# Value products of the prompt moved to the spare columns of a transpose bank, in a one-core hybrid decoder layer

## What is computed

```
q, k, v, z_b, u, v_a, z_a, g_a, g_b = split(x @ w_in + b_in)        # 2048 -> 17408 columns
branch A: y_a = gelu(u) * (tril(w_s) @ layer_norm(gelu(v_a)) + b_s) * silu(z_a)      # chunks of 128
branch B: 3 dilated windows (128,1), (512,4), (2048,16) of 8 heads x 128, rotary q and k;
          o = softmax(q k^T / sqrt(128)) v per window, the three merged by their softmax weights
          y_b = o_b * silu(z_b)
merged = sigmoid(g_a) * (y_a @ w_o_a) + sigmoid(g_b) * (y_b @ w_o_b)
x <- layer_norm(2**0.25 * x + merged @ w_out)
```

## The kernel before, in words

| step | engine | work |
|---|---|---|
| 3 + 4i | TensorE | `prompt_scores(i)`: scores into the two banks of `scp` (lines 866, 868) |
| 4 + 4i | VectorE | scale, mask and maximum out of `scp` into `sc` (line 1583), maximum and its negative (lines 1640, 1574) |
| 4 + 4i | ScalarE | Exp of `sc` (line 1254) |
| 8 + 4i | VectorE | `normalise`: `sc` times the reciprocal sum (lines 1579, 1580) |
| 10 + 4i | TensorE | six transposes of `sc` into `turn` (line 830): four into bank 0 (half 0), two into columns 0 to 255 of bank 1 (half 1) |
| 11 + 4i | ScalarE | both halves copied to `pt` (line 1036) |
| 13 + 4i | TensorE | `prompt_out(i)`: six matmuls of `pt` with the values (line 878), into columns 0 to 127 of `scp` |
| 14 + 4i | VectorE | the product times the gate, into `zt`, which the profile calls `qkv` (line 1646) |

## Time and profile before

### The profile page before, as it was taken

One profiled execution on the slowest core, in us unless ns is written; L12 is line 12 of the kernel. 1 busy time (PEld: TensorE's weight loads), 2 busy tenths in 40 slices (PEclk: granted clock), 3 DMA queues, 4 the chain that ended last, 5 costly groups with the idle time before them and its releaser, 6 DMA issues.

```text
span 2398.1 us, 43888 instructions
## 1 busy us (share of the span) xinstructions
PE 2295.2 (96%) x17409; PEld 2245.2 (94%) x17409; DVE 1602.6 (67%) x2107; ACT 910.6 (38%) x1320; POOL 254.8 (11%) x458
## 2 busy tenths in 40 slices
PE   7999999999999999999988998999899989999997
PEld 7999999999999999999978998899889988999996
DVE  8677867867777776777747675676566656553435
ACT  5444444444444444444433233333333432332221
POOL 0100000000000000000023221221221110001000
PEclk9999999999999999999999999999899999999998
DMA  5443343433434334344368766866775573344333
GB/s 176 132 131 108 115 135 96 130 110 114 133 100 128 106 118 131 102 148 122 107 209 256 217 194 202 237 204 193 217 224 169 174 228 110 120 124 129 107 102 113
DMA packets 400521, 357.94 MB, mean 149 GB/s; under 512 B 15851, under 2 KB 360043, under 8 KB 398667
## 3 DMA queue, kind: packets, MB, share of 16 engines
q1 hardware_dynamic: 363168, 206.28, 29.5%
q0 software_dynamic: 37168, 148.95, 19.5%
HBM read 308.75 MB, written 46.41 MB: 148 GB/s over the span
## 4 chain that ended last, share of the span: by engine, by line
PE 81%; DMA 8%; DVE 6%; issue 2%; ACT 2%; SPq 0%; DVEq 0%; ACTq 0%
PE acc L738 47%; PE acc L810 25%; DMA raw<-in_w_in 5%; PE scp L892 2%; PE scp L878 1%; DMA cache<-in_cache_v 1%; DVE prod L1558 1%; DVE wl L1354 1%; PE acc L790 1%; PE turn L747 1%; DMA raw<-in_w_o_b 1%; ACT wh L1036 1%; PE scp L866 1%; PE turn L830 1%; DVE far L1559 1%
## 5 line engine op out<-in xcount | busy, mean ns | idle before, releaser
L738 PE MATMUL acc<-xh,wph 128*128 128x288 f32 x2856 | 850.0, 298 | 8.6 <-issue 7.9
L738 PE MATMUL acc<-xl,wph 128*128 128x288 f32 x2856 | 842.6, 295 | 0.0
L738 PE MATMUL acc<-xh,wpl 128*128 128x288 f32 x2856 | 839.6, 294 | 0.0
L738 PEld LDWEIGHTS acc<-xh,wph 128*128 128x128 f32 x2856 | 535.3, 187 | 10.4 <-issue 9.3
L738 PEld LDWEIGHTS acc<-xh,wpl 128*128 128x128 f32 x2856 | 537.8, 188 | 0.0
L738 PEld LDWEIGHTS acc<-xl,wph 128*128 128x128 f32 x2856 | 536.4, 188 | 0.0
L1354 DVE TENSOR_TENSOR wl<-raw,wh 128x512 fp32r<-128x512 f32 x256 | 176.6, 690 | 374.9 <-ACT wh L1036 374.0
L1036 ACT ACTIVATE wh<-raw 128x512 fp32r<-128x512 f32 x256 | 160.9, 629 | 562.2 <-PE acc L810 453.0
L810 PE MATMUL acc<-xh,wh 128*128 128x288 f32 x1024 | 239.8, 316 | 8.5 <-DVE wl L1354 8.5
L810 PE MATMUL acc<-xl,wh 128*128 128x288 f32 x1024 | 223.8, 300 | 0.0
L810 PE MATMUL acc<-xh,wl 128*128 128x288 f32 x1024 | 223.4, 300 | 0.0
(11 more groups left out here) (233 smaller groups left out, 3576.2 us busy)
## 6 DMA issues: line engine op xcount, KB each, us to landing
raw<-in_w_in SPq DMA_DIRECT2D x128, 256.0 KB, 4.6
cache<-in_cache_v POOLq DMA_DIRECT2D x64, 448.0 KB, 5.1
w_a<-in_w_in SPq DMA_DIRECT2D x52, 512.0 KB, 3.8
w_c<-in_w_in SPq DMA_DIRECT2D x52, 512.0 KB, 3.8
w_b<-in_w_in SPq DMA_DIRECT2D x52, 512.0 KB, 4.1
w_d<-in_w_in SPq DMA_DIRECT2D x52, 512.0 KB, 4.2
ones<-in_ones_k POOLq DMA_DIRECT2D x64, 256.0 KB, 3.8
raw<-in_w_out SPq DMA_DIRECT2D x64, 256.0 KB, 2.7
```

The costliest lines, as they stand in the source:

```text
L738: done = pe.matmul(bank, w[ring][:, k, :], a[x][:, k, :], start=(j in (0, 1, 3, 5) and k == 0 and t == 0), stop=(k == HK - 1 and t == 2), ...
```

## The change

Three things are changed.

1. The prompt's value product of each tile goes to columns 256 to 383 of `turn` bank 1 (`pv_at`) instead of `scp`. `("pv", i)` leaves the list `SCORES`, so TensorE no longer waits there for the scores to have been read. Two semaphores of their own, `out_scored` and `tile_read`, connect product and reader. Since bank 1 is now shared, the transposes of half 1 of tiles 1 to 3 (and of the sample's second half) wait until VectorE has read the product before. The product moves from step 13 + 4i to 12 + 4i, its reader from 14 + 4i to 13 + 4i.
2. The far-key sums at steps 13 and 17 move to 14 and 18.
3. At the branch `mix(g)` moves one quarter on, and `mixed`, `round_ya`, `split_ya` one iteration each; the last `round_ya` and `split_ya` fall into the first iteration of the `w_o_a` stage.

```diff
 def slot_pv(i):
-    return 13 + 4 * i
+    return 12 + 4 * i
-SLOT_ONES = [28, 38, 0, 2, 5, 9, 13, 17]
+SLOT_ONES = [28, 38, 0, 2, 5, 9, 14, 18]
-SCORES = ["early", ("qk", 0), ("qk", 1), ("qk", 2), ("pv", 0), ("qk", 3), ("pv", 1),
-          ("pv", 2), "far", ("pv", 3), "cached_pv", "sample_out"]
+SCORES = ["early", ("qk", 0), ("qk", 1), ("qk", 2), ("qk", 3), "far", "cached_pv", "sample_out"]
...
+        pv_at = turn[:, 1, 2 * P:3 * P]
...
+                elif name == ("pts", 1):
+                    pe.wait_ge(tile_read, 4 * f)
+                elif name[1] > 0:
+                    pe.wait_ge(tile_read, 4 * (f - 1) + name[1])
                 for cols, src, rows, width in pairs_:
...
                 def prompt_out(i):
-                    bank_free(("pv", i))
-
                     pe.wait_ge(turn_read, turn_no(f, ("pt", i, 1)))
                     for n in range(6):
                         g, tile = (0, n) if n < 4 else (n - 3, i)
-                        done = pe.matmul(scp[:, 0:P], vN[par][g][:, tile, :], pt[:, n * P:(n + 1) * P],
+                        done = pe.matmul(pv_at, vN[par][g][:, tile, :], pt[:, n * P:(n + 1) * P],
                                          start=(n == 0), stop=(n == 5))
-                    done.then_inc(scored, 1)
+                    done.then_inc(out_scored, 1)
...
-                        g, odd = divmod(2 * n + v - 15, 2)
+                        g, odd = divmod(2 * n + v - 16, 2)
                         if odd == 0 and 0 <= g < HEADS:
                             mix(g)
...
-                            act.wait_ge(scored, signal_no(f, ("pv", i - 1)))
+                            act.wait_ge(out_scored, 4 * (f - 1) + i)
...
-                        act.wait_ge(scored, signal_no(f, ("pv", 3)))
+                        act.wait_ge(out_scored, 4 * f)
...
-                g, odd = divmod(t - 17, 2)
+                g, odd = divmod(t - 18, 2)
                 if odd == 0 and 0 <= g < HEADS:
                     round_ya(g)
...
+                if t == 0:
+                    round_ya(HEADS - 1)
...
                             if s == slot_pv(i) + 1:
-                                dve.wait_ge(scored, signal_no(f, ("pv", i)))
+                                dve.wait_ge(out_scored, 4 * (f - 1) + i + 1)
                                 cols = slice(i * P, (i + 1) * P)
-                                v.tensor_tensor(zt[par][:, cols], scp[:, 0:P], zt[par][:, cols], ALU.mult
-                                                ).then_inc(score_read, 1)
+                                v.tensor_tensor(zt[par][:, cols], pv_at, zt[par][:, cols], ALU.mult
+                                                ).then_inc(tile_read, 1)
...
-                g, odd = divmod(t - 16, 2)
+                g, odd = divmod(t - 17, 2)
                 if g >= 0:
                     split_ya(g) if odd else mixed(g)
...
                 if t == 0:
+                    split_ya(HEADS - 1)
                     merge(Q_B, 15, 0)
```

More of the change, by code:

```diff
@@ L319, in build @@
         scored, score_read = sem("scored"), sem("score_read")
+        out_scored, tile_read = sem("out_scored"), sem("tile_read")
         v_in = [sem(f"v_in{i}") for i in range(4)]
@@ L1687, in frame @@
                             dve.wait_ge(score_read, score_no(f, "sample_out"))
+                            dve.wait_ge(tile_read, 4 * f)
                             v.tensor_tensor(zt[par][:, SEQ:TOK], otmp[:], zt[par][:, SEQ:TOK], ALU.mult).then_inc(y_done, 1)
```

## The result

The changed kernel takes 2370.01 us (median of 4 runs, 2366.61 to 2375.36), the kernel before, run beside it, 2394.22 (4 runs). The forecast's 14.5 us lie outside the interval of the first set (18 to 29 us) and inside that of the second (12 to 27). The profiled execution took 2371.65 us, its span is 2370.0. Both kernels have the same 17409 matmuls, so TensorE's time can differ only by idleness and by how fast it runs them.

A forecast was written before the change was run, and what follows sets the result against it. TensorE, busy 2295.2 of 2398.1 us, bounds the kernel, so only its waits can go. Frames 10.4 plus branch 5.4 make 15.8 us, lowered to 14.5 for an ordinary execution: 2393.84 - 14.5 = 2379.3 us, range 2371 to 2389.

The forecast's parts named there:

- The branch, 5.4: Ahead of the first mixing product: 3.2 us of idleness go and 2.2 us of slow clock.
- The wait for the read of the scores goes: At the value products: of 15.0 us of waits for VectorE's read of the scores, 12.2 are won.
- The product a step earlier, 2.4: At value products whose copied probabilities are late, waits grow: 2.4 us lost, with 0 and 4 as ends.
- The cover, "a wait up to about 3.05 us vanishes": At the value products: 1.60 us go with 1.45 of cover left; longer waits keep their excess.
- The shared bank, only its waits: At the second half of the transposes: costs only waits for the product's read, covered by 1.45 us.
- The far-key sums, "nothing": Sums a step on: no cost, on VectorE they only change places with the read of the product.
- Given back, 2.0 at the transposes of tile 3: In the two frames with long waits TensorE arrives earlier, VectorE doesn't: 1.0 us each, 2.0 lost.
- The clock, 2.6: Behind the two long waits at value products, matmuls no longer run at half clock: 2.6 us won.
- 15.0 - 0.2 - 1.0 - 1.6 = 12.2: Value products' waits for the read of the scores, less what stays of three long ones: 12.2 us won.
- the frames give it back: Rival: VectorE stays late, waits at line 830 replace those at the value products; frames give 2 us, 2386.4; chance 0.17.
- Late weights, slower: Rival: in frames 2, 4 and 6 TensorE meets late weight rests earlier; 14 us slower, 2407.8; chance 0.05.
- The branch does not do what it says: Rival: VectorE's full chain delays the mixing product; branch gives 1.5 us, frames 9.2, 2383.1; chance 0.08.

The follow-up runs named there:

- e1: The kernel before, unchanged, run again for a second trace: 2390.17 us, ratio 0.9991.
- e2: The kernel before with only the mixing product, its reads and its roundings a quarter on: 2387.93 us, ratio 0.9979.
- e11: The changed kernel, unchanged, run again for a second trace: 2373.78 us, ratio 0.9918.
- e5: The changed kernel with the branch undone, so the frames' changes alone: 2372.94 us, ratio 0.9917.
- e18: e12 with one weight load held back in frames 3, 5, 7 and 8, behind ScalarE's copy and ahead of VectorE's mask: 2400.09 us, ratio 1.0040.
- e19: e13 with the same four weight loads held back as in e18: 2393.93 us, ratio 1.0011.
- e7: The kernel before with the value product in the transpose bank, all steps as before: 2388.27 us, ratio 0.9991.
- e4: e5 with the far-key sums back at steps 13 and 17: 2384.02 us, ratio 0.9975.
- experiment 4: The kernel before with only the far-key sums moved to steps 14 and 18: 2390.8 us, ratio 0.9984.
- light pairs': Kernel before against the frames' changes alone, both with fewer loads, in two versions (e8 and e9, e12 and e13): differences 5.2 and 5.6 us.
- e15: e12 with one weight load held back in each of frames 2 to 8, ahead of ScalarE's copy: 2408.24 us, ratio 1.0083.
- e12: The kernel before with one of three groups of q, k and v loaded from the third head on: 2374.43 us, ratio 0.9934.
- e16: e13 with the same weight loads held back as in e15: 2403.95 us, ratio 1.0070.
- e13: The frames-only kernel e5 with the same loads taken out as in e12: 2368.86 us, ratio 0.9910.
- e14: The changed kernel with its first far-key sum moved from step 28 to step 30: 2355.29 us, ratio 0.9877.
- e8: The kernel before with fewer q, k, v loads and mostly quarter far-key tiles: 2371.97 us, ratio 0.9930.
- e9: The frames-only kernel e5 with the same traffic taken out as in e8: 2366.77 us, ratio 0.9906.

## Why the prediction was off, step by step

The mechanism was the one forecast, and so was the branch; the terms of the frames were mis-sized. TensorE's idleness in the frames stage by what it waited for, mean of three traces each (before, e1, e2, and after, e11, e5), in us:

| wait | old frames | new frames |
|---|---|---|
| value products, for the read of the scores | 17.2 | 0 |
| value products, for the copy or the product before | 1.5 | 3.3 |
| transposes, for normalised scores of prompt and samples | 6.1 | 2.5 |
| transposes, for the read in the shared bank | none | 1.5 |
| cached products, "issue" | 5.2 | 11.9 |
| all others | 9.6 | 9.2 |
| idle in all | 39.6 | 28.4 |

- **The branch, 5.4: right.** Alone it gave 5 us by the times, and 5.2 by its stage over four traces each. The 0.26 us ahead of quarter 16 is as worked out, the mixing product waited 0.84 instead of 1.14, the slow clock behind it went, and `w_o_a` paid nothing.
- **The wait for the read of the scores goes: right, but undersized.** No wait of that kind is left. The forecast took 15.0 us and let 2.8 of it stay, 12.2; 17.2 went.
- **The product a step earlier, 2.4: about right.** The other waits of the products rose by 1.8 us.
- **The cover, "a wait up to about 3.05 us vanishes": right.** From the rows of e18 and e19 it is 3.64 - 0.71 = 2.93. Of the 3.25 and 4.02 us 0.3 and 1.1 would have stayed, where I had 0.20 and 0.97. What takes over stands at the transposes of the next tile. The second half waits for the product's read as forecast; ahead of it the first half waits for the normalised scores, which I had not named. It also came by itself, in frame 8 of e11 (3.17 + 0.49 us) and of e5 (0.31 + 0.95).
- **The shared bank, only its waits: right, if the sums move too.** 1.0 us in after. The Trainium skill, "PSUM — Partial Sum Buffer", section on bank collisions, has the hardware neither arbitrate nor stall; no run here puts two engines at the bank at once, so none tests it. What the bank costs is decided by the order on the reader's engine: 22.5 us (e7), 17.4 (e4), 2.0 (e5), 1.0.
- **The far-key sums, "nothing": right for themselves, but not harmless to leave.** Their move is what makes the rest work (e4 against e5, 14 us). I had said that they only change places with the read, and not that this is what the cover of 1.45 us rests on.
- **Given back, 2.0 at the transposes of tile 3: the size too small, the place wrong.** It was 9.6 us at the cached products between the two profiled executions (13.7 against 4.1), 6.7 in the mean of three traces each, and 1.5 more at the shared bank. TensorE's gain of a frame meets there a VectorE that is no earlier, 2.4 us of sum in front. My own test, "wrong if waits at the cached products grow by more than 5 us", was met, while the time came out better than forecast: the test looked at one side of the account.
- **The clock, 2.6: undersized or luck.** Busy time fell by 5.2 us in the mean. The slow clock at the frames' ends has no part in it (it costs 5.9 us a trace with the old frames and 6.3 with the new), and what has is not separated.
- **The step that failed: "15.0 - 0.2 - 1.0 - 1.6 = 12.2" for the waits of the frames, with "part of its late weights is probably its own" behind it.** I read one execution, took its late weights for partly its accident, left the waits at the transposes (line 830) in both kernels, and lowered 15.8 to 14.5. Over three traces each, the frames stage fell from 660.5 us to 644.2: 16.3, of which 11.1 are idleness and 5.2 busy time, where the sum had 10.4. In the sum's terms: the waits of the products gave 17.2 - 1.8 = 15.4, not 12.2 - 2.4 = 9.8; the transposes' waits for normalised scores gave 3.6, not 0; the busy time 5.2, not 2.6; given back were 6.7 + 1.5 = 8.2, not 2.0. That makes 16.0 instead of 10.4. That the forecast is no further off is in part luck, since errors of 5.6, 3.6 and 2.6 us stand against one of 6.2.

Where the surplus comes from is shown in part. Shown: it depends on the traffic, since with lighter loads the pair differs by 5.2 and 5.6 us where it differed by 20. Without most late tiles the old products wait only 9.2 and 9.5 us; the 8 us above that came with late tiles. Shown: for a tile late between copy and mask the new order absorbs 2.9 us more, and such tiles stand in before (frames 3 and 7) and e1 (frames 3 and 7). Shown: for a tile late ahead of the copy it absorbs nothing more. Frame 2 is such a place: the product of tile 1 waits the lateness less 4.24 us in the old order (5.93 - 1.69 in before, 7.91 - 3.67 in e1) and less 3.76 in the new (4.52 - 0.76 in e11). But the tile was 5.9, 7.9 and 10.9 us late in the three old traces, and in time, 4.5 and 7.1 us late in the three new ones; that is worth 2.6 us in the mean (4.0 of waiting against 1.4), and whether the new order brings it about or the executions happened to differ is open. So are the 3.6 us at the transposes, which vary from 0.6 to 10.2 between the old traces. Less lateness in sum is no explanation (experiment 4). Open, too, is how much of the light pairs' small difference is TensorE's speed: idleness there still differs by 7.1 and 2.6 us, but busy time by 4.9 us the wrong way in the one pair and 1.2 us the right way in the other.

Of the rivals, "the frames give it back" had its mechanism right (6.7 us at the cached products in the mean) and its size and place wrong. "Late weights, slower" had the sign wrong: held-back tiles cost both orders about alike, by the ratios 36 us in e15 over e12 and 38 in e16 over e13. "The branch does not do what it says" fell.

## What to carry to other kernels

When a wait is taken off a pipelined schedule, follow the faster engine to the next place where it meets the slower one, over the whole period and not the next few steps, and look what stands just ahead of the awaited instruction there: here a 2.4 us sum that could as well stand behind it, worth 6 to 10 us by the ratios where the change is worth 20 to 24. Waits caused by late transfers are part of a kernel's ordinary time even where their sizes change from one execution to the next, so price a cover against their distribution over several traces, not against one. Where a cover is measured, add up all the waits that take over, up to the point where the engine runs on. And take edits that hand a buffer over together with the order on the engine that reads it: by the ratios the bank alone changed the time by -2 us, the sums alone by -4, step and sums without the bank by +6, bank and step without the sums by -6, and all three together by -20.

## What the runs showed of the hardware

TensorE's clock fell to half without any idleness ahead of it. Each frame ends with 16 products of 8 columns (line 902 before, `scp<-fold,osm`, about 2 us in which the engine counts as busy), and in the full parts behind them the granted clock was 0.50 to 0.65 in some frames and 1.00 in others. The end of frame 1 of before on TensorE, where no row shows a wait, then 3 us windows of frame 1 and frame 2:

```profile
1324.64 0.88 PE L899 MATMUL scp<-psn,qkv 64*128 64x64 f32 x6
1325.45 2.25 PE L902 MATMUL scp<-fold,osm 16*128 16x8 f32 x16
1327.63 0.85 PE L810 MATMUL acc<-xh,wh 128*128 128x288 f32 x2
1328.28 0.68 PE L810 MATMUL acc<-xl,wh 128*128 128x288 f32 x2
```
```profile
1328.00:1331.00 3.00, 3.00 (x14) 3.00 (x14) 1.24 (x4) 1.26 (x2) 0.54 (x1) 0.50 0.54 186
1414.40:1417.40 3.00, 3.00 (x25) 2.83 (x24) 1.98 (x3) 1.26 (x2) 0.54 (x1) 1.00 0.71 226
```

Fourteen matmuls instead of 25 in the same 3 us. This happened in 4 of 8 frames in before, after and e14, in 5 of e1, in 6 of 8 in e2, e5 and e11, in 3 of e8 and in 7 of e9. From the first of the 16 products to the end of the three parts behind it are 4.47 us where the clock stayed up and 5.3 to 6.9 where it fell, 1.4 us more on average. Between after and e11, the same kernel, this makes 3.4 of the 5.0 us by which the busy time of the stage differs, with no instruction changed: single traces of this kernel can't be compared finer than some 5 us in busy time; idle time is not free of such accidents either (35.9 to 42.5 us in three traces of the old frames). That it is the 8-column products that bring the clock down, and not the 16-column ones a little ahead of them, is not shown. The Trainium skill, "TensorE: Matmul & The Clock Gate", section on the clock gate, says of the start of a kernel that the count of matmuls at the low clock varies from run to run; the frames above show such a variation in the middle of one.
